# Head squares summed from a rounded and a low part, two places later in the projection

## The chip, the cores and the metric

One Trainium2 chip, one core of it. The metric is device time in microseconds (us) of that core from launch to end, the median of the runs shown. TensorE does matrix products into PSUM, VectorE and ScalarE do element-wise work, GpSimd does some more of it in SBUF alone, SyncE issues the DMAs. Each engine takes its instructions in the order in which they were written; semaphores order them against each other.

## The reference, cut to what matters

A trunk layer: a normalised and modulated input is projected to 20 tiles of 128 features. Four heads run a gated linear attention forward and backward, beside a short convolution and a pooling. The sum of both directions, `o` (128 features for each of 1024 tokens and each head), is normalised over its own 128 features and gated. Then come the output projection and a large MLP.

```
def gla_out(o, r, norm_w):
    o = o * lax.rsqrt(jnp.mean(o * o, axis=-1, keepdims=True) + EPS) * norm_w.astype(jnp.float32)
    bsz, h, n, dv = o.shape
    o = o.transpose(0, 2, 1, 3).reshape(bsz, n, h * dv)
    return (o * jax.nn.silu(r.astype(jnp.float32))).astype(r.dtype)
```

The change is in how the mean of `o * o` is made.

## The kernel before

Features lie on the partitions, tokens along the free dimension. All large products are made of rounded operands: `a_hi` and `w_hi` are copies rounded to the format F32R, `a_lo` and `w_lo` are what the rounding left, and a product is `w_hi*a_hi + w_hi*a_lo + w_lo*a_hi`. ScalarE makes `w_hi` for the next weight tile (L1540), VectorE makes `w_lo` (L2149).

The projection runs over the tiles of `PROJ` (L957), one tile of 128 features after the other, each over 8 contraction blocks. A block is six matmuls of 128x512: three products for each half of the tokens. The results alternate between the two halves of the PSUM tensor `main`. Into this stream a table, `PLAN`, puts the small work: `put(tile, slot, job)` runs a job behind contraction block `slot` of tile `tile`. I number these places as 8 x tile + slot. Every engine walks through the same table and issues its own part of each job, so one table sets the order of TensorE, ScalarE and VectorE. Three rules matter here. At the start of its tile ScalarE rounds the next weights, ahead of the tile's jobs; at slot 3 VectorE makes their low part, ahead of the slot's jobs; and behind the last job of a tile each engine works on what the tile itself made (for a gate tile `R` on ScalarE: L1708, L1709, L1710; for `CC` L1700; on VectorE for `CH` L2318 to L2323).

The jobs, with their lines:
- `A`, head and half: scores. TensorE L1127 into `sm`; VectorE masks them (L2212) and adds both directions to `a_sum` (L2218).
- `O`: outputs of a head and a half. TensorE L1149 and L1154 into `ob`. ScalarE squares `ob` once both halves are there (L1629), into `sqo`.
- `ns`, head and half: the sum of squares over the 128 features, spread over all partitions, as one FP32 product of 128x128 ones with 512 tokens of `sqo` (TensorE L1161, into `sm`). ScalarE makes the inverse root as exponential of a logarithm (L1488 reads `sm` and frees it, L1494). VectorE multiplies the outputs by it, once for both halves (L2224).
- `u`: state updates (TensorE L1109; ScalarE copies them out of `sm`, L1611, L1613). `ch`: VectorE's chain over the forward states (L2203). GpSimd runs the backward chain (L828, L831), outside the table. `mx`: ScalarE scales the states (L1620) that `O` reads.
- `pl`: the pooling's small product (TensorE L1168; ScalarE L1640). Its input `ypool` is finished by GpSimd (L853, L854).
- `rl`, `rg`: the gate. VectorE L2333, ScalarE's sigmoid L1714, then VectorE L2339 and L2341.

The tensor `sm` has two banks, used in turn by all these jobs in the order of the table; a job may write a bank only after the job two before it has been read (`begin_small`). The outputs of a head also wait for the multiplication of the head before (`y_normed`).

Head `h` has its outputs at `OUT_AT[h]` = 80, 96, 113, 124 and two places later. GpSimd's input for the pooling product of places 86 and 87 is made in tile 10, which is that of head 0's outputs.

Of the kernel before, what the change touches and what calls it, by code (L numbers as in the profile page):

```python
# [21 lines left out]
P = 128  # L22
# [109 lines left out]
for _h in range(HEADS):  # L132
    put_all(CHAIN_AT[_h], 2, ("ch", _h, 0), ("ch", _h, 1), ("ch", _h, 2))
    put_all(MIX_AT[_h], 1, ("mx", _h, 0), ("mx", _h, 1))
    for _d in range(2):
        put_all(HEAD_AT[_h], 2, ("A", _h, 0, _d), ("A", _h, 1, _d))
    put_all(OUT_AT[_h], 2, ("O", _h, 0), ("O", _h, 1))
    put_all(OUT_AT[_h] + 4, 1, ("ns", _h, 0), ("ns", _h, 1))
    _r = PROJ.index(f"R{_h}") + 1
    put(_r, 3, "rl", _h)  # L140
    put(_r, 5, "rg", _h)
    if _h >= 2:
        for _n in range(2):
            put_all(UPD_AT[_h], 2, ("u", _h, _n), ("u", _h, 2 + _n))
# [57 lines left out]
def hybrid_trunk(nc, wstream, wg_in, wm1, wm2, xt, ct, small_in, gw_in, out):  # L202
    ctx = ExitStack()
    with ctx:
        cursor = [(nc.sbuf_base + 63) // 64 * 64]

        def at(name, shape, dt, offset):
            return nc.alloc_sbuf_tensor_at(name, shape, dt, offset=offset)
# [94 lines left out]
        macc = at("macc", [P, N], F32, ZF + 5 * KIB)  # L303
        scaled_state = at("scaled_state", [P, DV], F32, ZF + 9 * KIB + 256)
        mbuf_late = at("mbuf_late", [P, 4, N], F32, ZD)
# [6 lines left out]
        sqo = at("sqo", [P, N], F32, ZF + 10 * KIB)  # L312
        rso = at("rso", [P, N], F32, ZF + 14 * KIB)

        early_hi = at("early_hi", [P, 2, N], F32R, ZA)
# [107 lines left out]
        o_done = sem("o_done")  # L423
        sqo_made = sem("sqo_made")
        rso_made = sem("rso_made")
        y_normed = sem("y_normed")
# [517 lines left out]
        def _(pe):  # L944
# [213 lines left out]
            def head_sums(h, i):  # L1158
                b = begin_small(("ns", h, i))
                pe.wait_ge(sqo_made, h + 1)  # L1160
                pe.matmul(sm[:, b, :], ones, sqo[:, i * HALF:(i + 1) * HALF], start=True, stop=True).then_inc(small_done, 1)  # L1161

# [319 lines left out]
        def _(act):  # L1482
# [140 lines left out]
            def outputs(h, i):  # L1623
                if i == 1:
                    act.wait_ge(o_done, 2 * (h + 1))
                    act.wait_ge(summed, 2)
                    if h >= 1:
                        act.wait_ge(y_normed, h)
                    act.activation(sqo[:, :], ob[:, :], ACT.Square).then_inc(sqo_made, 1)  # L1629

            def head_sums(h, i):
# [447 lines left out]
        def _(dve):  # L2079
# [141 lines left out]
            def head_sums(h, i):  # L2221
                if i == 1:
# [3 lines left out]
                    dve.wait_ge(y_normed, h + 1)  # L2226

            def mod_product(g):
                s = S_OF[("md", g)]
# [6 lines left out]

            jobs = {"ch": chain_states, "A": scores, "ns": head_sums, "md": mod_product}

# [603 lines left out]
```

## Time and profile before

| | us |
|---|---|
| median of 3 runs | 1082.21 |
| lowest and highest | 1081.92, 1082.45 |
| span of the profiled execution | 1081.0 |
| TensorE matmuls in flight | 1056.2 (98%) |
| VectorE busy | 824.0 (76%) |
| ScalarE busy | 510.8 (47%) |
| GpSimd busy | 307.5 (28%) |

The span is from the first to the last instruction of one execution; the time of a run also has what lies around it. A matmul's duration in the trace includes its way through the array, so neighbours overlap: what one costs is read from the distance of starts. A row of the timeline merges neighbours of one kind; in brackets stands the idle time ahead of it and who ended it.

### The profile page before, as it was taken

Reading aid. Unit: us, or ns where it says so; the run is one execution under the profiler, and the core shown is the slowest. Engines: PE = TensorE matmul, PEld = TensorE weight load, DVE = VectorE, ACT = ScalarE, POOL = GpSimd, SP = SyncE. Lnnn points to the kernel's source line nnn. Section 1 sums busy time; section 2 is a strip of 40 time slices with the busy share of each in tenths; the row PEclk is TensorE's granted clock in tenths of the full one; section 3 lists DMA queues with packets and bytes.
Section 4 is the critical chain, followed back from the end, with each engine's and each line's share of the span. In section 5 each row is a group of like instructions: output and inputs, shape, how many; then the busy total and the mean of one; then the engine's idle time right before and its main releaser. Section 6 shows DMA issues by size and latency. Waiting matters only on the chain.

```text
span 1081.0 us, 16409 instructions
## 1 busy us (share of the span) xinstructions
PE 1056.2 (98%) x5566; PEld 850.7 (79%) x5566; DVE 824.0 (76%) x1062; ACT 510.8 (47%) x827; POOL 307.5 (28%) x280
## 2 busy tenths in 40 slices
PE   8999999999999999999999999999999999999995
PEld 4688888777778888887888888888788888888883
DVE  5878868646445986899787787878987777787776
ACT  6665443356525123576766666666422222222234
POOL 1000006487101452012332423233322231222222
PEclk9999999999999999999999999999999999999998
DMA  9733331101013664226766565768745854774604
GB/s 338 260 111 104 117 117 40 40 21 40 21 59 116 263 233 146 78 98 251 308 247 260 224 269 229 269 236 312 291 170 221 349 205 181 314 278 184 237 1 156
DMA packets 66646, 199.82 MB, mean 185 GB/s; under 512 B 5664, under 2 KB 15136, under 8 KB 66592
## 3 DMA queue, kind: packets, MB, share of 16 engines
q1 hardware_dynamic: 66592, 199.11, 49.7%
q8 instruction: 33, 0.54, 0.2%
q14 instruction: 21, 0.17, 0.0%
HBM read 139.32 MB, written 59.77 MB: 184 GB/s over the span
## 4 chain that ended last, share of the span: by engine, by line
PE 49%; DVE 4%; issue 1%; POOL 0%; DVEq 0%; ACT 0%; ACTq 0%; POOLq 0%
PE ob L1410 13%; PE main L1452 13%; PE sm L1410 10%; PE sm L1452 8%; PE ob L1452 6%; DVE XR L2680 1%; DVE XR L2747 1%; DVE stage L2561 1%; DVE slot L2511 1%; DVE slot L2506 0%; DVE stage_last L2561 0%; DVE t_tmp L2554 0%; DVE hid L2568 0%; DVE t_tmp L2545 0%; POOL raw L918 0%
## 5 line engine op out<-in xcount | busy, mean ns | idle before, releaser
L957 PE MATMUL main<-a_hi,w_hi 128*128 128x512 f32 x376 | 125.8, 416 | 0.0
L1410 PE MATMUL ob<-h_sum,slot 128*128 128x512 f32 x504 | 122.5, 392 | 2.3 <-DVE hid L2568 2.1
L1881 ACT ACTIVATE slot<-raw 128x512 fp32r<-128x512 f32 x80 | 50.2, 631 | 153.1 <-PE main L1452 58.4
L957 PE MATMUL main<-a_lo,w_hi 128*128 128x512 f32 x376 | 116.5, 391 | 0.0
L957 PE MATMUL main<-a_hi,w_lo 128*128 128x512 f32 x376 | 116.2, 390 | 0.0
L1410 PEld LDWEIGHTS ob<-h_sum,slot 128*128 128x128 f32 x504 | 95.2, 189 | 22.9 <-issue 2.5
L2680 DVE SCALAR_TENSOR_TENSOR XR<-main,mods,XR 128x512 f32<-128x512 f32 x112 | 83.3, 748 | 28.8 <-PE main L1452 27.7
L957 PEld LDWEIGHTS main<-a_lo,w_hi 128*128 128x128 f32 x376 | 70.6, 188 | 15.5
L957 PEld LDWEIGHTS main<-a_hi,w_lo 128*128 128x128 f32 x376 | 70.6, 188 | 15.5
L957 PEld LDWEIGHTS main<-a_hi,w_hi 128*128 128x128 f32 x376 | 66.7, 188 | 17.9 <-issue 5.8
L1452 PE MATMUL main<-t_even,slot 128*128 128x512 f32 x336 | 78.1, 389 | 0.0
L2506 DVE TENSOR_TENSOR slot<-raw,slot 128x512 fp32r<-128x512 f32 x70 | 62.5, 894 | 18.5 <-ACT slot L1869 18.5
L1410 PE MATMUL sm<-h_hi,slot 128*128 128x512 f32 x224 | 73.5, 389 | 0.0
L1452 PEld LDWEIGHTS main<-t_even,slot 128*128 128x128 f32 x336 | 63.1, 188 | 13.1
L828 POOL TENSOR_TENSOR scaled_state<-tst,decay 64x128 f32<-64x128 f32 x60 | 29.0, 483 | 146.2 <-ACT tst L1613 141.7
L2511 DVE TENSOR_TENSOR slot<-raw,slot 128x512 fp32r<-128x512 f32 x80 | 61.3, 781 | 0.2 <-ACT slot L1881 0.2
L2680 DVE SCALAR_TENSOR_TENSOR XR<-sm,mods,XR 128x512 f32<-128x512 f32 x64 | 47.7, 748 | 13.3 <-PE sm L1452 12.4
L918 POOL TENSOR_TENSOR raw<-part_sum,raw 128x512 f32<-128x512 f32 x16 | 21.0, 1312 | 122.3 <-DVE slot L2511 122.3
L889 POOL TENSOR_TENSOR held<-raw 128x512 f32<-128x512 f32 x14 | 23.3, 1663 | 108.4 <-DMA raw<-wstream 60.3
L897 POOL TENSOR_TENSOR held<-raw 128x512 f32<-128x512 f32 x14 | 24.6, 1756 | 90.9 <-DVE slot L2506 90.9
L2680 DVE SCALAR_TENSOR_TENSOR XR<-ob,mods,XR 128x512 f32<-128x512 f32 x48 | 35.8, 749 | 18.4 <-PE ob L1452 18.3
L1410 PEld LDWEIGHTS sm<-h_hi,slot 128*128 128x128 f32 x224 | 42.1, 188 | 8.7
(338 smaller groups left out, 2442.1 us busy)
## 6 DMA issues: line engine op xcount, KB each, us to landing
hidden_kept<-stage SPq DMA_DIRECT2D x98, 512.0 KB, 4.3
raw<-wstream SPq DMA_DIRECT2D x60, 512.0 KB, 4.2
t_even<-hidden_kept SPq DMA_DIRECT2D x56, 512.0 KB, 5.7
raw<-wstream SPq DMA_DIRECT2D x16, 1024.0 KB, 5.4
stage<-hidden_kept SPq DMA_DIRECT2D x21, 512.0 KB, 5.5
stage_last<-hidden_kept SPq DMA_DIRECT2D x21, 512.0 KB, 6.4
wmod<-wm SPq DMA_DIRECT2D x8, 1024.0 KB, 12.8
mbuf<-wm SPq DMA_DIRECT2D x16, 512.0 KB, 4.0
```

The lines of the kernel that those rows point to most:

```text
L828: pool.tensor_tensor(scaled_state[DK:P, :], tst[DK:P, h % 2, c, :], decay[DK:P, h, c:c + 1].broadcast_to([DK, DV]), ALU.mult).then_inc(sta ...
L889: pool.tensor_tensor(sums, a21, a22, ALU.add).then_inc(w1_sum, 1)
L897: pool.tensor_tensor(sums, a12, a11, ALU.subtract).then_inc(w1_sum, 1)
L918: pool.tensor_tensor(a11, sums, a11, ALU.subtract).then_inc(w2_sum, 1)
L957: ins = pe.matmul(main[:, bank, half * HALF:(half + 1) * HALF], w[:, slot, k, :], x[:, half * HALF:(half + 1) * HALF], start=begin, stop=end)
L1410: ins = pe.matmul(hid_bank(acc, odd), slots1[j][:, w, kp, :], parts[x][:, kp, :], start=PARTS[j][3] and kp == 0 and m == 0, stop=kp == KP ...
L1452: ins = pe.matmul(product_bank(s, acc, q), slots2[j][:, w, q, kp, :], tset[odd][j][kp][:, x, :], start=begins and kp == 0 and n == 0, stop ...
L1881: act.activation(slots2[j][:, 0, :, :, :], operand(s, j), ACT.Copy).then_inc(w2_hi, 1)
L2506: tt(slots1[j][:, 1, :, :], operand1(b, j), slots1[j][:, 0, :, :].bitcast(F32), ALU.subtract).then_inc(w1_lo, 1)
L2511: tt(slots2[j][:, 1, :, :, :], operand(s, j), slots2[j][:, 0, :, :, :].bitcast(F32), ALU.subtract).then_inc(w2_lo, 1)
L2561: tt(y[:, 1, :], sources(odd)[j], y[:, 0, :].bitcast(F32), ALU.subtract).then_inc(t_lo, 1)
L2680: stt(out=XR[m][:, cols], in0=product_bank(s, acc, q), scalar=mods[:, 3, m:m + 1], in1=XR[m][:, cols], op0=ALU.mult, op1=ALU.add).then_inc ...
```

## The change

Per head, three things change.

1. The squares are split as the other operands are. ScalarE rounds `sqo` to `sqo_hi`, right behind the squares. VectorE makes `sqo_lo = sqo - sqo_hi` in a new job, `sl`, at the place where the first sum used to be. In head 0 ScalarE also rounds the ones once (`ones_r`).
2. A sum is two products of `ones_r`, with `sqo_hi` and with `sqo_lo`, in place of one FP32 product.
3. The two sums of a head move two places later: from 84, 85 / 100, 101 / 117, 118 / 128, 129 to 86, 87 / 102, 103 / 119, 120 / 130, 131. ScalarE's and VectorE's parts of `ns` move with them.

`sqo_lo` lies where `sqo` lies and `sqo_hi` where the inverse root is written later; the ones take a place beside GpSimd's `scaled_state`, which moves by 256 bytes. No DMA is added or moved.

```diff
-    put_all(OUT_AT[_h] + 4, 1, ("ns", _h, 0), ("ns", _h, 1))
+    put_all(OUT_AT[_h] + 4, 1, ("sl", _h))
+    put_all(OUT_AT[_h] + 6, 1, ("ns", _h, 0), ("ns", _h, 1))
...
-                pe.wait_ge(sqo_made, h + 1)
-                pe.matmul(sm[:, b, :], ones, sqo[:, i * HALF:(i + 1) * HALF], start=True, stop=True).then_inc(small_done, 1)
+                pe.wait_ge(sqo_split, h + 1)
+                cols = slice(i * HALF, (i + 1) * HALF)
+                pe.matmul(sm[:, b, :], ones_r[:, :], sqo_hi[:, cols], start=True, stop=False)
+                pe.matmul(sm[:, b, :], ones_r[:, :], sqo_lo[:, cols], start=False, stop=True).then_inc(small_done, 1)
...
                     act.activation(sqo[:, :], ob[:, :], ACT.Square).then_inc(sqo_made, 1)
+                    act.wait_ge(sqo_made, h + 1)
+                    if h == 0:
+                        act.activation(ones_r[:, :], ones, ACT.Copy)
+                    act.activation(sqo_hi[:, :], sqo[:, :], ACT.Copy).then_inc(sqo_rounded, 1)
...
+            def square_low(h):
+                dve.wait_ge(sqo_rounded, h + 1)
+                tt(sqo_lo[:, :], sqo[:, :], sqo_hi[:, :].bitcast(F32), ALU.subtract).then_inc(sqo_split, 1)
```

TensorE in head 0, from the second of its output products on, before. A row `L957` with `x2` is a third of a contraction block; numbers in names are those of the allocation.

```order
L1161 MATMUL sm<-sqo_114,small_65 128x512 [waits sqo_made,small_free0]
L957 MATMUL main<-a_hi_52,w_hi_50 128x512 x2
L957 MATMUL main<-a_lo_53,w_hi_50 128x512 x2
L957 MATMUL main<-a_hi_52,w_lo_51 128x512 x2
L1161 MATMUL sm<-sqo_114,small_65 128x512 [waits sqo_made,small_free1]
...
L1168 MATMUL sm<-ypool_99,small_65 128x512 [waits masks_loaded,pooled,small_free0]
...
L1168 MATMUL sm<-ypool_99,small_65 128x512 [waits masks_loaded,pooled,small_free1]
```

And after, the same stretch:

```order
L1168 MATMUL sm<-sqo_hi_118,ones_r_107 128x512 [waits sqo_split,small_free0]
L1169 MATMUL sm<-sqo_lo_117,ones_r_107 128x512
L1176 MATMUL sm<-ypool_99,small_65 128x512 [waits masks_loaded,pooled,small_free1]
...
L1168 MATMUL sm<-sqo_hi_118,ones_r_107 128x512 [waits sqo_split,small_free0]
L1169 MATMUL sm<-sqo_lo_117,ones_r_107 128x512
L1176 MATMUL sm<-ypool_99,small_65 128x512 [waits masks_loaded,pooled,small_free1]
```

The sums used to stand one and two blocks ahead of the pooling products; now a sum stands directly in front of each.

ScalarE in head 2, from its squares on, before:

```order
L1629 ACTIVATE sqo_114<-ob 128x1024 [waits y_normed,summed,o_done]
L1714 ACTIVATE rsig_113<-rsig_113 128x1024 [waits r_min]
L1488 ACTIVATE rso_115<-sm,small_65 128x512 [waits small_done]
L1494 ACTIVATE rso_115<-rso_115 128x512 [waits small_free0]
L1488 ACTIVATE rso_115<-sm,small_65 128x512 [waits small_done]
L1494 ACTIVATE rso_115<-rso_115 128x512 [waits small_free1]
L1708 ACTIVATE rsig_113<-main 128x1024 [waits y_gated,pads_made,tile_done]
L1709 ACTIVATE rsig_113<-rsig_113 128x1024 [waits act_chain]
L1710 ACTIVATE rsig_113<-rsig_113,small_65 128x1024 [waits act_chain]
L1540 ACTIVATE w_hi_50<-raw_49 128x1024 [waits split_done,tile_done,raw_loaded0]
```

And after:

```order
L1637 ACTIVATE sqo_115<-ob 128x1024 [waits y_normed,summed,o_done]
L1641 ACTIVATE sqo_hi_118<-sqo_115 128x1024 [waits sqo_made]
L1726 ACTIVATE rsig_114<-rsig_114 128x1024 [waits r_min]
L1496 ACTIVATE rso_116<-sm,small_65 128x512 [waits small_done]
L1502 ACTIVATE rso_116<-rso_116 128x512 [waits small_free0]
L1720 ACTIVATE rsig_114<-main 128x1024 [waits y_gated,pads_made,tile_done]
L1721 ACTIVATE rsig_114<-rsig_114 128x1024 [waits act_chain]
L1722 ACTIVATE rsig_114<-rsig_114,small_65 128x1024 [waits act_chain]
L1548 ACTIVATE w_hi_50<-raw_49 128x1024 [waits split_done,tile_done,raw_loaded0]
L1496 ACTIVATE rso_116<-sm,small_65 128x512 [waits small_done]
L1502 ACTIVATE rso_116<-rso_116 128x512 [waits small_free1]
```

The second logarithm stands behind the gate's three operations and the rounding of the next weights; the new rounding stands in front of the sigmoid.

VectorE in head 1, from the last piece of its forward chain on, before:

```order
L2203 SCALAR_TENSOR_TENSOR tst_101<-tst_101,decay_69 64x128 [waits states_forward] x4
L2149 TENSOR_TENSOR w_lo_51<-raw_49,w_hi_50 128x1024 [waits hi_made]
L2224 TENSOR_TENSOR vtok_92<-ob,rso_115 128x8x128 [waits rso_made]
L2327 TENSOR_TENSOR yconv_100<-main,yconv_100 128x1024 [waits tile_done,y_normed]
```

And after:

```order
L2215 SCALAR_TENSOR_TENSOR tst_101<-tst_101,decay_69 64x128 [waits states_forward] x4
L2161 TENSOR_TENSOR w_lo_51<-raw_49,w_hi_50 128x1024 [waits hi_made]
L2242 TENSOR_TENSOR sqo_lo_117<-sqo_115,sqo_hi_118 128x1024 [waits sqo_rounded]
L2236 TENSOR_TENSOR vtok_92<-ob,rso_116 128x8x128 [waits rso_made]
L2343 TENSOR_TENSOR yconv_100<-main,yconv_100 128x1024 [waits tile_done,y_normed]
```

The low part of the squares stands behind the low part of the weights. In head 2 it stands behind the gate (L2355, L2357 after, L2339 and L2341 before).

## Rows read from the trace of the kernel before

**Rows 1.** The page: span, and TensorE's busy time.
```profile
span 1081.0 us, 16409 instructions
PE 1056.2 (98%) x5566; PEld 850.7 (79%) x5566; DVE 824.0 (76%) x1062; ACT 510.8 (47%) x827; POOL 307.5 (28%) x280
```

**Rows 2.** Timeline of TensorE, head 0: start, duration, line, operands, count, idle before.
```profile
208.85 0.62 PE L957 MATMUL main<-a_hi,w_hi 128*128 128x512 f32 x2
...
210.23 1.04 PE L1161 MATMUL sm<-sqo,small 128*128 128x512 f32 x2
...
214.74 1.02 PE L1168 MATMUL sm<-ypool,small 128*128 128x512 f32 x2
```

**Rows 3.** Timeline of ScalarE, head 0 and the state copies behind it.
```profile
209.00 1.03 ACT L1629 ACTIVATE sqo<-ob 128x1024 f32<-128x1024 f32 x1 [7.29 <-DVE ypool L2311]
...
218.04 0.69 ACT L1640 ACTIVATE ypool<-sm,small 128x512 f32<-128x512 f32 x1 [1.56 <-PE sm L1168]
...
222.83 0.59 ACT L1613 ACTIVATE tst<-sm 64x512 f32<-64x512 f32 x1
```

**Rows 4.** Timeline of GpSimd: the pooling's last operation, two of the chain.
```profile
212.50 2.02 POOL L854 TENSOR_TENSOR ypool<-ypool,upad 128x1024 f32<-128x1024 f32 x1
...
247.11 1.47 POOL L828 TENSOR_TENSOR scaled_state<-tst,decay 64x128 f32<-64x128 f32 x1
...
249.19 0.40 POOL L828 TENSOR_TENSOR scaled_state<-tst,decay 64x128 f32<-64x128 f32 x1
```

**Rows 5.** Timeline of TensorE, head 1: outputs, first sum, state products.
```profile
234.95 0.69 PE L1149 MATMUL ob<-a_sum,vtok 64*64 64x64 f32 x32 [0.18 <-ACT tst L1620]
...
244.19 1.02 PE L1161 MATMUL sm<-sqo,small 128*128 128x512 f32 x2
...
248.79 1.16 PE L1109 MATMUL sm<-vtok,ktok 64*128 64x128 f32 x16
...
252.82 1.16 PE L1109 MATMUL sm<-vtok,ktok 64*128 64x128 f32 x16
```

**Rows 6.** Timeline of VectorE, head 1.
```profile
236.84 0.69 DVE L2218 TENSOR_TENSOR a_sum<-a_f,a_b 128x512 f32<-128x512 f32 x1 [2.43 <-PE ob L1154]
...
247.10 1.21 DVE L2149 TENSOR_TENSOR w_lo<-raw,w_hi 128x1024 fp32r<-128x1024 f32 x1
```

**Rows 7.** Timeline of TensorE, heads 2 and 3: first sums, scores between.
```profile
280.28 1.10 PE L1161 MATMUL sm<-sqo,small 128*128 128x512 f32 x2 [0.97 <-ACT sqo L1629]
...
286.31 0.69 PE L1127 MATMUL sm<-qe,ku 64*64 64x64 f32 x32
...
302.71 1.02 PE L1161 MATMUL sm<-sqo,small 128*128 128x512 f32 x2
```

**Rows 8.** Timeline of ScalarE, head 2.
```profile
279.13 1.00 ACT L1629 ACTIVATE sqo<-ob 128x1024 f32<-128x1024 f32 x1
280.04 1.04 ACT L1714 ACTIVATE rsig<-rsig 128x1024 f32<-128x1024 f32 x1
281.41 0.69 ACT L1488 ACTIVATE rso<-sm,small 128x512 f32<-128x512 f32 x1 [0.33 <-PE sm L1161]
...
285.05 1.03 ACT L1708 ACTIVATE rsig<-main 128x1024 f32<-128x1024 f32 x1
...
288.26 1.04 ACT L1540 ACTIVATE w_hi<-raw 128x1024 fp32r<-128x1024 f32 x1
```

**Rows 9.** Timeline of VectorE, the gates behind heads 2 and 3.
```profile
282.37 1.28 DVE L2341 SCALAR_TENSOR_TENSOR vtok<-vtok,small,rsig 128x1024 f32<-128x1024 f32 x1
...
300.81 1.29 DVE L2341 SCALAR_TENSOR_TENSOR vtok<-vtok,small,rsig 128x1024 f32<-128x1024 f32 x1
```

**Rows 10.** Stretches: busy time by engine (count), then TensorE's granted clock, DMA.
```profile
1070.00:1072.00 2.00, 0.00 (x0) 0.00 (x0) 2.00 (x5) 1.12 (x2) 0.80 (x1) 1.00 1.03 382
1072.00:1075.00 3.00, 0.00 (x0) 0.00 (x0) 2.66 (x5) 1.44 (x2) 1.70 (x2) 0.56 1.01 382
```

More of the change, by code:

```diff
@@ L303, in hybrid_trunk @@
         macc = at("macc", [P, N], F32, ZF + 5 * KIB)
-        scaled_state = at("scaled_state", [P, DV], F32, ZF + 9 * KIB + 256)
+        scaled_state = at("scaled_state", [P, DV], F32, ZF + 9 * KIB)
+        ones_r = at("ones_r", [P, P], F32R, ZF + 9 * KIB + 512)
         mbuf_late = at("mbuf_late", [P, 4, N], F32, ZD)
@@ L313, in hybrid_trunk @@
         rso = at("rso", [P, N], F32, ZF + 14 * KIB)
+        sqo_lo = at("sqo_lo", [P, N], F32R, ZF + 10 * KIB)
+        sqo_hi = at("sqo_hi", [P, N], F32R, ZF + 14 * KIB)
         early_hi = at("early_hi", [P, 2, N], F32R, ZA)
@@ L424, in hybrid_trunk @@
         sqo_made = sem("sqo_made")
+        sqo_rounded = sem("sqo_rounded")
+        sqo_split = sem("sqo_split")
         rso_made = sem("rso_made")
@@ L2235, in mod_product @@
                     link(stt(out=gain2[:, :], in0=mods[:, 2, :], scalar=1.0, in1=col("n2"), op0=ALU.add, op1=ALU.mult))
-            jobs = {"ch": chain_states, "A": scores, "ns": head_sums, "md": mod_product}
+            jobs = {"ch": chain_states, "A": scores, "sl": square_low, "ns": head_sums, "md": mod_product}
             def gates(j):
```

## The prediction

> **What bounds the kernel now.** I read the head of the page first: the span is 1081.0 us and TensorE has matmuls in flight for 98% of it [rows 1]. So matmul time is time, and every wait put in front of TensorE is time too, unless a wait behind it shrinks. Everything the change touches lies between 205 and 310 us, so I then read TensorE's timeline there. A contraction block of the projection (six rounded matmuls) takes 210.23 - 208.85 = 1.38 us, thus a pair of rounded 128x512 matmuls 1.38 / 3 = 0.46. From 210.23 to 214.74 stand two blocks and two FP32 sums, so an FP32 128x512 matmul costs (4.51 - 2 x 1.38) / 2 = 0.87 [rows 2]. Last I read ScalarE, VectorE and GpSimd in the same stretch [rows 3, 4, 6, 8, 9], because the new operands of the sums come from two of them, through queues that run in order. All times below are on the trace's axis; a "shift" is how much later TensorE is than before.
>
> **What it removes.** Eight FP32 sums, 8 x 0.87 = 7.0 us on TensorE's path. It adds eight pairs of rounded ones, 8 x 0.46 = 3.7. Alone that is 8 x 0.41 = 3.3 us faster. The one wait for the squares that the trace has, 0.97 us in head 2 [rows 7], could go as well.
>
> **What it adds.** Per head: a ScalarE copy that rounds the squares, 1.04 us (the copy of a weight tile has the same shape [rows 8]), in head 0 also the rounding of the 128x128 ones (no such row: above 0, below the 0.69 of a 128x512 operation [rows 8]; I take 0.3, and it decides nothing below); then a VectorE subtraction, 1.22 us by the low part of the weights, same shape and types [rows 6]. The last is queued at the first of the four places, the sums two places later, so TensorE gives the chain 2 x 1.38 us more. The question is per head whether both queues are free by then.
>
> **Head 0 (places 84 to 87).** The squares run from 209.00 to 210.03 [rows 3], the ones to about 210.35, the rounded squares to 211.35, the low part to 212.6. TensorE without the sums comes to place 86 at 210.23 + 2 x 1.38 = 213.0: no wait for the sum. But at the same place the pooling product follows, and TensorE now asks for it at 213.5 instead of 214.74. Its input comes from GpSimd, whose last operation on it runs from 212.50 for 2.02 us, to 214.52 [rows 4]: a wait of 1.1 us that the two FP32 sums had covered. And VectorE's subtraction reads two SBUF tensors while GpSimd works. Such a subtraction (247.10, 1.21 us [rows 6]) stretched the GpSimd operation beside it from 0.40 to 1.47 us [rows 4], so I take 1.1 us more: input ready at 215.6, product at 215.7, shift +1.0. With one sum (0.46) now between the two pooling products the second stands at 215.7 + 0.87 + 1.38 + 0.46 = 218.4. ScalarE copies it out behind its own logarithm and exponential of the sum: sum done 218.57, then 0.69 + 0.66, so the copy starts at 219.9 instead of 218.04 [rows 3]. From there ScalarE has no gap to 222.83 + 0.59 = 223.42, where TensorE's state product waits for its banks, so that product shifts by +1.85. The output product of head 1 had a wait of 0.2 us of its own (234.95 [rows 5]), whose releaser, GpSimd's chain, moves by only 1.1: the wait vanishes. Shift there: +1.6.
>
> The Trainium skill, GPSIMD Engine Reference, section 8 (Key points), says that GpSimd shares its SBUF interfaces with VectorE and that VectorE instructions with two SBUF inputs contend. The rows of 247.10 agree; by this rule the shift at the pooling product is +1.0, and without it -0.1, which makes the whole sum about 1.1 us smaller.
>
> **Head 1 (places 100 to 103).** VectorE's queue is what is late. From 236.84, when the first output product frees it, it works without a gap to the low part of the weights at 247.10 [rows 6], and the new subtraction stands behind that one: 248.24 to 249.46. TensorE comes to place 102 at 244.19 + 2.76 = 246.95 [rows 5], so it waits 2.5 us, to 249.5. Behind the sum at this place are the state products, for which ScalarE must first have read the sum's bank: 249.5 + 0.62 + 0.03 + 0.69 (logarithm [rows 8]) = 250.85, where TensorE is free at 250.06: 0.8 us more. They start at 250.9; the next ones follow after 252.82 - 248.79 = 4.03 us [rows 5] plus the second sum, 0.46: 255.4 instead of 252.82, +2.6. Shift: +4.2. GpSimd's chain for head 2's outputs starts on those products, so it moves along.
>
> **Head 2 (places 117 to 120).** On the axis of before: squares at 279.13 to 280.13 (ScalarE is late from the scaled states, whose chain moves along), rounded squares to 281.2, then the sigmoid of the first gate, which was at 280.04 [rows 8], from 281.1 to 282.15. VectorE gates head 0 behind that (its first operation lies between 281.08 and 282.37, its second ends at 283.65 [rows 9]), now +1.07: 284.7. Only then comes the subtraction, to 285.9. TensorE, at place 117 at 280.28 - 0.97 = 279.31, comes to 119 at 282.1: a wait of 3.8 us. Worse is the split over two tiles: the sum of place 119 is the last job of its tile, that of place 120 the first of the next. ScalarE's order has the three gate operations and the rounding of the next weights between their logarithms (shown word for word in the section on the change). They took from 285.05 to 289.30 [rows 8]. Now: first sum at 285.9, logarithm and exponential to 287.9, the block of 4.25 us to 292.0, second logarithm to 292.65. TensorE issued the second sum at 287.7, and directly behind it stands the score product of head 3, which needs that bank: from 288.3 it waits 4.4 us, to 292.7 instead of 286.31 [rows 7]. Shift: +6.4.
>
> **Head 3 (places 128 to 131).** Squares at about 299.9, rounded by 302.1; VectorE's gate ends at 302.10 [rows 9], low part by 303.3. TensorE comes to place 130 at 302.71 + 2.76 = 305.5 [rows 7]: no wait, and 2 x 0.41 = 0.8 us are gained.
>
> **Sum.** 1.6 + 2.6 + 6.4 - 0.8 = +9.8 us. After that TensorE is the bound again, and what is later on it is later at the end. Against the profiled execution's own span: 1081.0 + 9.8 = 1090.8. The median of the runs shown, 1082.21, lies 1.2 above that span; so **1092.0 us**, +0.9%.
>
> **Rivals.**
> *All of it stays covered* (faster). The low part would have to be written before TensorE reaches the sum in every head, and the second logarithm before the score product. Then -3.3, with head 2's wait gone -4.3: 1078 to 1079. For it: the lead of two places, 2.76 us, is longer than either new operation, and heads 0 and 3 keep it. Against it: the queues above. It decides at 246.95 in head 1 (VectorE is busy to 248.3) and at 282.1 in head 2. 4%.
> *GpSimd is not held up by the new subtraction.* Head 0 then costs 0.5 instead of 1.6: 1090.9. 15%.
> *Only one of head 2's waits counts*: if the second logarithm finds ScalarE free, 4.4 us fall away: 1087.6. The order speaks against it. 7%.
> *The clock falls.* The end of the trace has TensorE idle: the granted clock is still 1.00 (2.4 GHz) in the two us from 1070, 0.56 on average in the three from 1072, with no matmul in either [rows 10]. Head 2's two waits, 3.8 and 4.4 us, are the first such gaps between matmuls in this kernel. A fall in the first costs nothing, since the 2.3 us of work up to the second would be hidden by it at 1.2 GHz too; one in the second costs 1.38 us for each contraction block run at half clock. How many those are no row shows; one to four give 1.4 to 5.5, I take 2: 1094. 29%. The Trainium skill, TensorE: Matmul & The Clock Gate, section Why this matters for your kernels, says that idle gaps between bursts of matmuls bring the half clock back. No row inside the kernel tests it. By that rule this rival's 1094 would be the forecast, by the trace's middle 1092.
>
> **Numbers.** The forecast of 1092.0 has 45%, as GpSimd held, both of head 2's waits, no fall. The range must hold the GpSimd and the clock cases and a size of ScalarE's block that is off by a microsecond: 1088.5 to 1095.5; it leaves out the covered case, the one-wait case and the top of the clock case. A difference of 0.2% (2.2 us) is about what a measurement of this kernel can tell from none. Slower 0.93, within 0.02, faster 0.05.
>
> **What would show it.** In the profile after: rounded sums at 0.46 us a pair; a TensorE wait of 1 to 2.5 us on GpSimd's pooling in head 0; one of about 2.5 on VectorE's low part and one of 0.8 on a logarithm in head 1; 3.8 and 4.4 in head 2, the second released by ScalarE's logarithm; none in head 3. TensorE's matmul time should be 3.3 us less and its idle time some 13 us more. I am wrong if VectorE reaches the low part of head 1 before 247 us, if ScalarE makes the second logarithm of head 2 before the gate block, or if the wait for the banks was already there in another form.

## The result and the profile after

The changed kernel takes **1098.01 us** (median of 4 runs, 1096.19 to 1098.84), beside 1082.18 (1081.92 to 1082.45) for the kernel before in the same comparison: a ratio of 1.0143, 95% interval 1.0132 to 1.0155. That is 15.8 us slower, where +9.8 was forecast: the sign was right, the size lies outside the range. The profiled execution is the one of 1096.19; its span is 1094.4, 13.4 longer than that of before.

The page of the changed kernel: the span, busy time by engine, and the granted clock of TensorE in 40 slices.

```profile
span 1094.4 us, 16417 instructions
...
PE 1059.1 (97%) x5566; PEld 854.7 (78%) x5566; DVE 830.2 (76%) x1066; ACT 514.4 (47%) x832; POOL 309.5 (28%) x280
...
PEclk9999999999799999999999999999999999999998
```

The forecast was 3.3 us less matmul time than in [rows 1]. There are 2.9 more, and one slice (the eleventh, 274 to 301 us) has a clock of 0.7. TensorE's idle time, span less busy, went from 24.8 to 35.3. So two things are to be found: which waits came, and where the clock went.

The waits of the changed kernel between 130 and 340 us: who waited for whom, the sum, how often, the longest.

```profile
DVE rsig L2355 <- ACT rsig L1726: 8.2, 2, 7.1
...
PE sm L1168 <- DVE sqo_lo L2242: 7.1, 3, 4.0
...
PE sm L1133 <- issue: 2.8, 1, 2.8
...
PE sm L1115 <- issue: 1.3, 2, 0.8
```

TensorE waits three times for the low part of the squares. "issue" says that the profile shows no releaser; the order tells it (a bank that ScalarE has to read first). The wait of VectorE's gate in it, 7.1 us at the longest, comes back below. Now the same places as in [rows 2, 5, 7]: TensorE's timeline after, heads 0 to 3 (start, duration, line, operands, count, idle before).

```profile
213.32 0.47 PE L1168 MATMUL sm<-sqo_hi,ones_r 128*128 128x512 f32 x1 [0.56 <-DVE sqo_lo L2242]
213.62 0.39 PE L1169 MATMUL sm<-sqo_lo,ones_r 128*128 128x512 f32 x1
213.86 1.02 PE L1176 MATMUL sm<-ypool,small 128*128 128x512 f32 x2
...
235.23 0.69 PE L1155 MATMUL ob<-a_sum,vtok 64*64 64x64 f32 x32 [0.47 <-ACT tst L1628]
...
249.88 0.47 PE L1168 MATMUL sm<-sqo_hi,ones_r 128*128 128x512 f32 x1 [2.52 <-DVE sqo_lo L2242]
...
251.40 1.23 PE L1115 MATMUL sm<-vtok,ktok 64*128 64x128 f32 x16 [0.82 <-issue]
...
290.69 0.77 PE L1168 MATMUL sm<-sqo_hi,ones_r 128*128 128x512 f32 x1 [4.00 <-DVE sqo_lo L2242]
...
298.06 1.13 PE L1133 MATMUL sm<-qe,ku 64*64 64x64 f32 x32 [2.77 <-issue]
...
319.68 0.39 PE L1168 MATMUL sm<-sqo_hi,ones_r 128*128 128x512 f32 x1
319.90 0.39 PE L1169 MATMUL sm<-sqo_lo,ones_r 128*128 128x512 f32 x1
```

The difference of starts to [rows 5, 7] is the shift: the first output product of head 1 is 0.28 late, the scores of head 3 are 11.75 late (298.06 against 286.31). In head 3 the two rounded products of a sum start 0.22 apart and nothing waits. Who holds the low part in heads 1 and 2 stands in VectorE's timeline after.

```profile
247.39 1.21 DVE L2161 TENSOR_TENSOR w_lo<-raw,w_hi 128x1024 fp32r<-128x1024 f32 x1
248.52 1.21 DVE L2242 TENSOR_TENSOR sqo_lo<-sqo,sqo_hi 128x1024 fp32r<-128x1024 f32 x1
...
286.86 1.22 DVE L2355 TENSOR_TENSOR rsig<-main,rsig 128x1024 f32<-128x1024 f32 x1 [7.05 <-ACT rsig L1726]
288.12 1.28 DVE L2357 SCALAR_TENSOR_TENSOR vtok<-vtok,small,rsig 128x1024 f32<-128x1024 f32 x1
289.33 1.22 DVE L2242 TENSOR_TENSOR sqo_lo<-sqo,sqo_hi 128x1024 fp32r<-128x1024 f32 x1
```

In head 1 it stands behind the low part of the weights, in head 2 behind the gate. VectorE had stood still 7.05 us for ScalarE's sigmoid, so it was not busy there, only queued in the wrong order. And who holds the scores of head 3: ScalarE's timeline after, between the two logarithms of head 2.

```profile
291.92 0.69 ACT L1496 ACTIVATE rso<-sm,small 128x512 f32<-128x512 f32 x1 [5.09 <-PE sm L1169]
...
293.17 1.00 ACT L1720 ACTIVATE rsig<-main 128x1024 f32<-128x1024 f32 x1
...
296.35 1.04 ACT L1548 ACTIVATE w_hi<-raw 128x1024 fp32r<-128x1024 f32 x1
297.30 0.67 ACT L1496 ACTIVATE rso<-sm,small 128x512 f32<-128x512 f32 x1
```

The second logarithm ends at 297.97, and the scores start at 298.06. Last the clock: stretches of the changed kernel, with busy time of TensorE, its weight loads, VectorE, ScalarE and GpSimd, then the granted clock (1.00 is 2.4 GHz, 0.50 is 1.2) and DMA.

```profile
253.00:255.00 2.00, 2.00 (x6) 1.52 (x6) 0.00 (x0) 1.86 (x4) 0.00 (x0) 0.50 0.00 0
...
256.00:260.00 4.00, 4.00 (x29) 3.12 (x28) 2.39 (x2) 3.57 (x6) 0.00 (x0) 1.00 0.00 0
286.00:290.00 4.00, 0.69 (x4) 0.22 (x2) 3.10 (x3) 0.83 (x1) 0.00 (x0) 0.99 0.00 0
290.00:300.00 10.00, 6.54 (x44) 4.89 (x45) 1.85 (x3) 6.58 (x8) 0.00 (x0) 0.50 0.00 0
300.00:303.00 3.00, 3.00 (x8) 2.32 (x8) 2.08 (x3) 0.00 (x0) 0.00 (x0) 0.50 0.00 0
...
304.00:310.00 6.00, 6.00 (x112) 4.81 (x112) 1.89 (x3) 0.00 (x0) 0.00 (x0) 1.00 0.01 3
```

It fell twice. Behind head 1's gaps (2.52, then 0.82) it was at half for some three microseconds, when TensorE was at work again: the contraction block at 252.56 took 2.73 us instead of 1.38. In head 2 it fell at the end of the first gap and stayed at half through the second one and some five microseconds beyond the start of the scores (298.06; 0.50 to 303). The forecast had named such a fall as a rival, in head 2 only, at 2 us.

A span also holds what differs ahead of the change. The last wait of TensorE that no kernel here alters (0.80 us, for the masks) ends at 196.04 in the kernel before and at 195.69 in the changed one, and between 195.65 and 196.86 in those below. So I also give, for each kernel, how much later than before TensorE comes to the first matmul of the MLP (439.88 us in the kernel before), counted from the end of that wait: its lateness, 13.7 us in the changed kernel. It comes from one execution, as a span does, but it leaves out what differs ahead of the change and in the MLP.

### The profile page after: what moved, and what is told of

Read it like the earlier page. It is cut to its first block, busy times and chain, and to the rows that moved or that the text cites. A ratio compares the mean times of both kernels' runs of the same rounds, so it can differ in the third digit from the quotient of the medians.

```text
span 1094.4 us, 16417 instructions
## 1 busy us (share of the span) xinstructions
PE 1059.1 (97%) x5566; PEld 854.7 (78%) x5566; DVE 830.2 (76%) x1066; ACT 514.4 (47%) x832; POOL 309.5 (28%) x280
## 4 chain that ended last, share of the span: by engine, by line
PE 48%; DVE 4%; issue 1%; POOL 0%; DVEq 0%; ACT 0%; ACTq 0%; POOLq 0%
PE ob L1418 13%; PE main L1460 12%; PE sm L1418 10%; PE sm L1460 8%; PE ob L1460 5%; DVE XR L2696 1%; DVE XR L2763 1%; DVE stage L2577 1%; DVE slot L2527 1%; DVE slot L2522 0%; DVE stage_last L2577 0%; DVE t_tmp L2570 0%; DVE hid L2584 0%; DVE t_tmp L2561 0%; DVE t_tmp L2556 0%
## 5 line engine op out<-in xcount | busy, mean ns | idle before, releaser
L963 PEld LDWEIGHTS main<-a_lo,w_hi 128*128 128x128 f32 x376 | 71.7, 191 | 15.8
L818 POOL TENSOR_TENSOR w_hi<-raw,small 128x1024 fp32r<-128x1024 f32 x7 | 18.6, 2651 | 112.0 <-PE main L963 112.0
```

The costliest lines, as they stand in the source:

```text
L818: pool.tensor_tensor(w_hi[:, b, :, :], raw[:, b, :, :], ones.unsqueeze(1).broadcast_to([P, KT, P]), ALU.mult).then_inc(linked, 1)
L963: ins = pe.matmul(main[:, bank, half * HALF:(half + 1) * HALF], w[:, slot, k, :], x[:, half * HALF:(half + 1) * HALF], start=begin, stop=end)
```

## The experiments

The theory, **A**: the waits are those of the prediction (VectorE's order in heads 1 and 2, and ScalarE's between the two logarithms of head 2), and what is missing to 1098 is the price of the clock. The rival, **B**: the waits are longer in themselves, or work behind them is slower for another reason than the clock. The changed kernel and the ten of the experiments, each with the ratio to the kernel before as run beside it on the same chip. Span and lateness are those of the one profiled execution:

| kernel | what it is | median us (range, runs) | ratio (95%) | span | lateness |
|---|---|---|---|---|---|
| after | the change | 1098.01 (1096.19-1098.84, 4) | 1.0143 (1.0132-1.0155) | 1094.4 | 13.7 |
| e1_filled | spare matmuls in three waits | 1091.48 (1090.64-1091.94, 4) | 1.0074 (1.0057-1.0091) | 1090.2 | 9.0 |
| e8_fill_head2 | the same in head 2 alone | 1094.80 (1091.64-1095.26, 4) | 1.0107 (1.0089-1.0124) | 1092.6 | 10.6 |
| e2_move_only | places moved, no split | 1086.85 (1086.29-1088.34, 5) | 1.0034 (1.0019-1.0048) | 1086.5 | 6.2 |
| e3_split_only | split, places not moved | 1099.92 (1099.30-1101.21, 4) | 1.0157 (1.0139-1.0174) | 1097.9 | 17.5 |
| e5_head2_together | both sums of head 2 in one tile | 1090.93 (1088.01-1091.77, 4) | 1.0070 (1.0053-1.0087) | 1089.9 | 9.0 |
| e9_head1_only | low part of head 1 earlier | 1091.58 (1090.20-1092.76, 4) | 1.0084 (1.0066-1.0102) | 1089.3 | 8.5 |
| e10_head2_low_first | low part of head 2 ahead of the gate | 1091.82 (1090.83-1094.23, 4) | 1.0082 (1.0065-1.0099) | 1092.4 | 11.7 |
| e6_head1_low_early | both of these | 1087.97 (1087.85-1088.48, 4) | 1.0051 (1.0036-1.0066) | 1086.7 | 5.2 |
| e4_replaced | all places chosen by the queues | 1081.88 (1080.10-1083.91, 10) | 0.9993 (0.9983-1.0003) | 1078.7 | -0.8 |
| e7_mixed | as e4, head 0 in FP32 as before | 1080.95 (1079.67-1082.06, 11) | 0.9986 (0.9977-0.9995) | 1079.1 | -1.4 |

**Filling the waits.** The same dependences, but TensorE works in the long waits on products that nobody reads (into the bank that the next sum overwrites). Ten in head 1, 16 in head 2's first wait, 18 ahead of the scores of head 3.

```diff
-                banks = [begin_small(("A", h, i, e)) for e in range(2)]
+                banks = [begin_small(("A", h, i, 0))]
+                if h == 3 and i == 0:
+                    for _ in range(18):
+                        pe.matmul(sm[:, banks[0], :], a_hi[:, 0, 0:P], a_hi[:, 0, 0:HALF], start=True, stop=True)
+                banks.append(begin_small(("A", h, i, 1)))
...
+                if i == 0:
+                    for _ in range({1: 10, 2: 16}.get(h, 0)):
+                        pe.matmul(sm[:, b, :], a_hi[:, 0, 0:P], a_hi[:, 0, 0:HALF], start=True, stop=True)
```

> The changed kernel, with spare matmuls (rounded, 128x512, 0.23 us each, into a bank that is overwritten afterwards) where TensorE only waits: 10 ahead of head 1's first sum, 16 ahead of head 2's, 18 between head 2's second sum and head 3's scores. They add no work to the path if the waits are as long as in the profile after (2.5 and 4.0 us, and 4.4 by the prediction's sum at full clock). Theory A (waits plus a fallen clock): the granted clock stays 1.00 through 245 to 310 us and the time falls by what the half clock cost, 4.6 us of the profiled execution's 13.4 and up to 7 of the median's 15.8: about 1091. Rival B (waits alone, and they are longer than I summed them): the time stays at 1096 to 1098.

Measured: 1091.48, with a ratio of 1.0074 against 1.0143. The first sums of heads 1 and 2 and the scores of head 3 in its TensorE timeline:

```profile
250.25 0.50 PE L1175 MATMUL sm<-sqo_hi,ones_r 128*128 128x512 f32 x1 [0.16 <-DVE sqo_lo L2249]
...
289.45 0.50 PE L1175 MATMUL sm<-sqo_hi,ones_r 128*128 128x512 f32 x1 [0.30 <-DVE sqo_lo L2249]
...
296.34 0.69 PE L1137 MATMUL sm<-qe,ku 64*64 64x64 f32 x32 [0.25 <-ACT rso L1503]
```

And the stretch with head 2 of the same kernel (columns as above):

```profile
280.00:300.00 20.00, 19.45 (x116) 15.20 (x119) 6.56 (x7) 12.24 (x21) 0.00 (x0) 1.00 0.01 4
```

The sums still come when the low part is there (250.25 beside 249.88), so no dependence was shortened; all that changed is that TensorE did not stand still. The clock stays at 1.00, and 4.7 us of lateness (4.2 of span) and 6.5 of the median are gone (7.5 by the ratios). B is out for that part: more useless work made the kernel faster. The price of the clock is 4.7 us between the two profiled executions. The 6.5 to 7.5 over the runs are more than these two gaps are shown to cost: three of the four executions of the filled kernel have a mean granted clock of 0.997, its profiled one 0.994, which fits a fall in the MLP that comes and goes (see the part on the forecast). What is left, 8.0 us by the ratio, 8.8 by the medians of that comparison and 9.0 of lateness, is the price of the waits themselves. The Trainium skill, TensorE: Matmul & The Clock Gate, section Why this matters for your kernels, says that idle stretches between bursts of matmuls bring half the clock back; this pair of kernels agrees.

**Filling head 2 alone** tells what head 1's fall costs (the difference to the filled kernel).

```diff
-                    for _ in range({1: 10, 2: 16}.get(h, 0)):
+                    for _ in range({2: 16}.get(h, 0)):
```

> The changed kernel with spare matmuls in head 2's two waits only (16 and 18), none in head 1's. Theory A (each fall of the clock has its own price): head 1's fall stays, 0.50 from about 252.3 to 255.6 us, and costs 1.7; head 2's goes. 1091.5 + 1.7 = 1093.2. Rival B (only head 2's fall matters): 1091.5.

Measured: 1094.80. Its waits are 2.50, 0.82, 0.30 and 0.25. The stretches with head 1 and with all that follows:

```profile
250.00:262.00 12.00, 10.16 (x58) 7.99 (x59) 3.32 (x3) 8.51 (x15) 3.29 (x6) 0.86 0.13 45
280.00:345.00 65.00, 64.45 (x507) 52.15 (x506) 27.53 (x26) 28.27 (x42) 0.13 (x1) 1.00 0.13 44
```

Against the fully filled kernel head 1's fall costs 1.6 us of lateness, where 1.7 was expected, and head 2's then 3.1. (The spans say 2.4 and 1.8, but at 196 us already this kernel was 0.7 later than the filled one and 1.2 later than the changed one.) The medians say 3.3 and 3.2 (3.6 by the ratios for each). Both falls count. That the medians are above the traces is not explained: the four executions of this kernel lie between 1091.64 (clock 0.997) and 1095.26 (0.991), so a difference of two such medians is rough.

**The move alone**: FP32 sums as before, two places later (the difference to the kernel before).

```diff
-    put_all(OUT_AT[_h] + 4, 1, ("ns", _h, 0), ("ns", _h, 1))
+    put_all(OUT_AT[_h] + 6, 1, ("ns", _h, 0), ("ns", _h, 1))
```

> The kernel before with FP32 sums as they were, but two places later; no split. Theory A (the place in the two queues costs, not the split's work): head 1's state products wait 0.8 us for the logarithm; in head 2 the second logarithm stands behind the gate block, TensorE waits about 4 us in front of head 3's scores, minus the 0.97 that goes; +3.8 us, and 1.7 to 2.5 more if the clock falls in that gap: 1086 to 1088.5. Rival B (only the split costs, moving is harmless): 1081 to 1082.

Measured: 1086.85, as expected. Its one large wait:

```profile
289.72 1.13 PE L1127 MATMUL sm<-qe,ku 64*64 64x64 f32 x32 [3.94 <-issue]
```

And the stretch behind it:

```profile
290.00:295.00 5.00, 5.00 (x42) 4.01 (x38) 3.39 (x4) 0.28 (x1) 0.00 (x0) 0.50 0.00 0
```

So the places 119 and 120, one tile apart, make a wait of 3.94 us without any split, and the clock falls behind it. In head 1 only the wait of 0.82 for the sum's bank is left, and the clock stays at 1.00 there.

**The split alone**, the sums at their old places (the difference to the changed kernel, as in the following ones unless said).

```diff
-    put_all(OUT_AT[_h] + 6, 1, ("ns", _h, 0), ("ns", _h, 1))
+    put_all(OUT_AT[_h] + 4, 1, ("ns", _h, 0), ("ns", _h, 1))
```

> The changed kernel with the sums at their old places, the low part at the first of them. Theory A (the low part is ready when the queues allow it, whatever the place of the sum): TensorE waits 2.9, 5.3 and 6.6 us in heads 0, 1 and 2 and 0.6 in head 3 and has no wait for the second logarithm; with 3.3 of work and 0.97 of wait gone +11 us, plus 2 to 5 for falls of the clock: 1095 to 1098. Rival B (the lead of two places is what hurts, by the banks and the logarithms): 1080 to 1084.

Measured: 1099.92, two above the upper end. The waits for the low part in its TensorE timeline:

```profile
213.24 0.47 PE L1168 MATMUL sm<-sqo_hi,ones_r 128*128 128x512 f32 x1 [3.25 <-DVE sqo_lo L2242]
...
253.00 0.77 PE L1168 MATMUL sm<-sqo_hi,ones_r 128*128 128x512 f32 x1 [5.03 <-DVE sqo_lo L2242]
...
296.83 0.77 PE L1168 MATMUL sm<-sqo_hi,ones_r 128*128 128x512 f32 x1 [6.72 <-DVE sqo_lo L2242]
```

The one in head 3 is 0.61. By the ratios the split costs 17.0 us where it stood, the move 3.7 without it, and both together 15.5. The two places that the chain was given are worth 5.2 us to it (17.0 + 3.7 - 15.5), and the move takes 3.7 of these back. The waits are as expected: 15.6 in sum, less 3.3 of work and 0.97 of wait, is 11.3 beside the 11 of the expectation. The lateness is 17.5, so some 6 are left for the clock (an estimate), above the 2 to 5 that were allowed. It fell behind the 3.25 in head 0 as well (0.93 on average from 205 to 230, where the changed kernel has 1.00). No run isolates that fall.

**Head 2's sums in one tile** removes the split over two tiles.

```diff
+LOW_PLACE = (84, 100, 117, 128)
+SUM_PLACE = ((86, 87), (102, 103), (119, 119), (130, 131))
...
-    put_all(OUT_AT[_h] + 4, 1, ("sl", _h))
-    put_all(OUT_AT[_h] + 6, 1, ("ns", _h, 0), ("ns", _h, 1))
+    put_all(LOW_PLACE[_h], 1, ("sl", _h))
+    for _i in range(2):
+        put_all(SUM_PLACE[_h][_i], 1, ("ns", _h, _i))
```

> The changed kernel, but head 2's two sums both at place 119, the last of their tile; nothing else moves. Theory A (ScalarE's order): the second logarithm now stands ahead of the gate block, the wait in front of head 3's scores shrinks from 4.4 us (by the sum at full clock) to about 0.4, the wait of 4.0 for the low part stays. Waits and work 4 to 4.5 us less, and the stretch of half clock behind the first gap is no longer prolonged: 1090 to 1092. Rival B (the gap in front of the scores has another cause, the masks or the outputs): 1096 to 1098.

Measured: 1090.93. The wait of 4.05 for the low part stays, the one ahead of the scores is gone, and 7.9 us with it (by the ratios; 4.7 of lateness). That is more than the wait of 2.77: the work between the two waits was hidden by ScalarE's block and is no longer, but the half-clock stretch is shorter too (0.66 from 290 to 300, 1.00 from there). The second sum itself moves one block ahead too, but it was not what the scores waited for: in the changed kernel it ends as their wait of 2.77 begins. Its logarithm now stands ahead of the gate block. This settles who released them.

**Head 1's low part earlier**, at place 97, ahead of a piece of VectorE's chain. I first ran it with a sort rule that puts every low part first in its place. This moved head 2's ahead of the gate as well, which I had not seen: the kernel holds two edits, not one.

Against the experiment before:

```diff
-LOW_PLACE = (84, 100, 117, 128)
+LOW_PLACE = (84, 97, 117, 128)
...
-    _jobs.sort(key=lambda job: (job[0] != "O"))
+    _jobs.sort(key=lambda job: (job[0] not in ("O", "sl")))
```

(The sums are at their places of the changed kernel.)

> The changed kernel, but head 1's low part at place 97, ahead of VectorE's last piece of the forward chain; the sums stay at 102 and 103. Theory A (VectorE's queue): the wait of 2.5 us goes, the 0.8 for the logarithm stays, the clock no longer falls behind it (1.7 us less): 1093 to 1094, TensorE's granted clock 1.00 from 240 to 280 us. Rival B (a gap of 0.8 is enough for the clock, or the low part is late for ScalarE's sake): 1095 or more.

Measured: 1087.97, a miss by five or more. The two edits were then taken apart, with these sort rules:

```diff
+    _jobs.sort(key=lambda job: (job[0] != "O" and job != ("sl", 1)))
```

> The changed kernel with one thing moved: head 1's low part at place 97, ahead of VectorE's last piece of the forward chain. (The earlier experiment of that aim also put head 2's low part ahead of the gate at place 117, by its rule for the order within a place.) Theory A (each head's wait has its own cause in VectorE's queue): head 1's wait of 2.5 us and the fall of the clock behind it (1.7) go, head 2's wait of 4.0 stays: 1098.0 - 4.2 = 1093.8. Rival B (the earlier experiment's 10 us came from head 1 alone): 1088.

```diff
+    _jobs.sort(key=lambda job: (job[0] != "O" and job != ("sl", 2)))
```

> The changed kernel with one thing moved: at place 117 head 2's low part stands ahead of the gate on VectorE. Theory A: the wait for it shrinks from 4.0 to 0.65 us, 0.4 more waits for the gate's bank, the gap in front of the scores stays (4.1 us, ScalarE's gate block), with one fall of the clock behind it instead of the long one of 13 us: 5.8 us less, 1092.2; head 1's wait of 2.5 and its fall stay. Rival B (the gap in front of the scores takes over what is gained): 1096 or more.

(In the first of the two the low part of head 1 is at 97, in the second at 100 as in the change.) Measured: 1091.58 and 1091.82. Head 2 in the TensorE timeline of e10:

```profile
288.73 0.47 PE L1168 MATMUL sm<-sqo_hi,ones_r 128*128 128x512 f32 x1 [0.61 <-DVE sqo_lo L2242]
289.86 0.70 PE L963 MATMUL main<-a_hi,w_hi 128*128 128x512 f32 x2 [0.43 <-DVE rsig L2355]
...
296.06 1.13 PE L1133 MATMUL sm<-qe,ku 64*64 64x64 f32 x32 [4.12 <-issue]
```

Taking the low part out from behind the gate shortens the first wait from 4.00 to 0.61. Yet the first sum starts only 2.0 earlier than in the changed kernel (288.73 against 290.69), because TensorE came to it 1.4 later, mostly by head 1, where the clock stood low for six microseconds and not for three (shown in the last section). ScalarE's block starts with that sum, so the scores come 2.0 earlier as well, and the wait in front of them grows from 2.77 to 4.12. Of the expected 5.8 this execution shows 2.0. That the median met the expectation is luck as far as the trace goes: the other three executions are 1.8 to 3.4 shorter. Their mean granted clocks order them, 1090.83 at 0.994, 1091.21 at 0.992, 1092.42 at 0.990, and the profiled 1094.23 at 0.988.

In e9 the wait of 2.5 is gone, the waits of head 2 are the old ones (4.01 and 2.77), and yet it came 2.2 below the expectation. The clock in its head 2:

```profile
285.00:290.00 5.00, 3.45 (x8) 2.81 (x9) 1.40 (x2) 2.19 (x3) 0.00 (x0) 0.50 0.00 0
...
292.00:294.00 2.00, 0.08 (x5) 0.11 (x8) 0.00 (x0) 1.97 (x4) 0.00 (x0) 1.00 0.00 0
...
295.00:298.00 3.00, 3.00 (x9) 2.32 (x8) 2.90 (x4) 0.00 (x0) 0.00 (x0) 0.50 0.00 0
```

Here it came back within the second gap and fell again for some three microseconds, where in the changed kernel it was down without a break. The same two gaps had another price: from head 2's outputs to head 3's TensorE falls back by 8.7 us here and by 9.6 in the changed kernel. The expectation had taken head 2's price from the changed kernel's profile; that step does not hold. Nor does the rival that head 1 alone gave the 10 us. By the medians the two edits give 6.4 and 6.2 alone and 10.0 together (by lateness 5.2, 2.0 and 8.5), so they do not simply add up, in either measure.

**All places by the queues.** The low part goes where VectorE is free (84, 97, 116, 128), both sums of head 1 to 101 and both of head 2 to 119, and a low part goes first in its place (the rule of e6). The two tables against the changed kernel:

```diff
+LOW_PLACE = (84, 97, 116, 128)
+SUM_PLACE = ((86, 87), (101, 101), (119, 119), (130, 131))
```

> The changed kernel with other places: the low part of head 1 at 97, ahead of VectorE's last piece of the forward chain, that of head 2 at 116, ahead of the gate; both sums of head 1 at 101, ahead of the state products, both of head 2 at 119, so that both logarithms stand ahead of the gate block. Theory A (queues): waits of 0.6 and 0.35 in head 1, 0.35 and 0.4 in head 2, head 0 as after (+0.6), 3.3 of work and 0.97 of wait gone, clock never below 1.00: about 1081. Rival B (the split is dear wherever it stands, by VectorE's and ScalarE's work): 1088 or more.

Measured: 1081.88 (ratio 0.9993). Six waits of 0.25 to 0.66 are left (2.99 in sum), and the clock is at 1.00 in this stretch. TensorE comes to the MLP 0.8 us early, and the median shows 0.8. The span is 2.3 shorter, but 0.3 of that was there at 196 us and 1.1 comes in the MLP, where this execution lacks a fall of the clock that the profiled one of before has. Three of the six waits are head 0's, so in the last kernel head 0 was left as it was. Against this kernel, with head 0 left out of ScalarE's and VectorE's new parts too:

```diff
+SUM_PLACE = ((84, 85), (101, 101), (119, 119), (130, 131))
...
+                if h == 0:
+                    pe.wait_ge(sqo_made, 1)
+                    pe.matmul(sm[:, b, :], ones, sqo[:, cols], start=True, stop=True).then_inc(small_done, 1)
+                    return
```

> The places of the experiment before that put the low parts early and the sums of heads 1 and 2 together, but head 0 as in the kernel before: one FP32 product, at 84 and 85, no split. Theory A (in head 0 the VectorE subtraction and GpSimd's pooling hold each other up, 0.6 us more than the 0.8 that the rounded sums save there): about 0.6 us below that experiment, span about 1078.1, time about 1081, 0.1% faster than before. Rival B (head 0 is neutral): the same as that experiment, or 0.8 above it, if head 0's saving is real and its waits are absorbed.

Measured: 1080.95, ratio 0.9986 (0.9977 to 0.9995), the fastest of all, 1.4 us below the kernel before and little more than can be told from no change. It comes to the MLP 1.4 early, 0.65 ahead of e4, as theory A has it for head 0. The spans of the two (1079.1 and 1078.7) say the opposite only because this execution is 1.1 later at 196 us already, and the ratios overlap. Its whole stretch from 195 to 345:

```profile
195.00:345.00 150.00, 147.47 (x1317) 115.46 (x1316) 83.29 (x97) 75.28 (x126) 63.55 (x97) 1.00 0.15 54
```

## Why the forecast had the sign and not the size

**What it removes** (-3.3): right. In head 3, where nothing waits, the rounded products start 0.22 to 0.23 apart, and TensorE's shift falls from 14.25 to 13.35, by 0.9 where 0.8 was forecast.

**Head 0** (+1.6): wrong, it is +0.6 (0.28 on the axis, where the squares had started 0.35 earlier than in [rows 3]). The step that failed is "its input comes from GpSimd, whose last operation on it runs from 212.50". That operation works for the second group of pooling. GpSimd in the changed kernel:

```profile
196.52 2.36 POOL L860 TENSOR_TENSOR ypool<-ypool,upad 128x1024 f32<-128x1024 f32 x1
...
212.17 2.88 POOL L860 TENSOR_TENSOR ypool<-ypool,upad 128x1024 f32<-128x1024 f32 x1
```

The product at 213.86 started while the second of these ran (to 215.05); its input was there since 198.88. The kernel says so too: a pooling product waits for `pooled` to reach `i + 1`, and at places 86 and 87 `i` is 0, the first group. (In GpSimd's own order that group belongs to tile 10, as the section on the kernel before has it; in time it was done before head 0's first outputs.) I had taken the nearest operation by time and name. [rows 2] could not have told, since the product before started at 214.74, behind both. The hold-up itself was right (2.88 against 2.02 in [rows 4]), nobody waited for it. What came in its place were 0.56 for the low part, 0.48 at the state products and 0.47 at head 1's outputs.

**Head 1** (+2.6; waits 2.5 and 0.8): the waits are 2.52 and 0.82. The fall of the clock behind them was not in the step: 1.35 us in one block of this execution, 1.6 in all by e8.

**Head 2** (waits 3.8 and 4.4): 4.00 and 2.77. The second is shorter because TensorE did the work between the two at half clock and came later; it did not end earlier, as the forecast says of its clock rival. On the axis the scores start at 298.06, where the forecast's steps give 286.31 + 6.4 + 4.2 = 296.9. ScalarE's queue was read right, operation for operation.

**Head 3** (no wait, -0.8): right, and the last difference of 13.4 is there by the end.

**The clock** is the step that failed: the forecast's sum put it at nothing, and filling the waits gave 4.7 us back. The rival had the mechanism, but "I take 2" was too small, "head 2's two waits are the first such gaps" left out head 1's, "A fall in the first costs nothing" is not so (0.7 up to the scores), and at 29% it was not in the forecast. In the profiled execution: 9.8 forecast, +0.45 to head 2 (head 0 gives 1.0 back and the execution is 0.35 ahead from the start, head 1's fall takes more), +0.7 up to the scores (the sum and its logarithm start later at half clock), +2.5 behind them (the shift grows from 11.75 to 14.25 until the next output product), which makes 13.4. At full clock the steps are right in their sum: 9.8 less head 0's 1.0 is 8.8, and the filled kernel has 9.0 of lateness, +8.8 by the medians and 8.0 by its ratio. That one of these is equal to a tenth is luck.

"No row inside the kernel tests it" was wrong as well. Its rows stop at 310 us and go on at 1070. In between the trace of before has a gap and a fall of the clock behind it:

```profile
504.30 4.20 PE L1410 MATMUL ob<-h_sum,slot 128*128 128x512 f32 x12 [2.07 <-DVE hid L2568]
...
505.80:509.10 3.30, 3.30 (x9) 2.59 (x8) 3.27 (x5) 3.27 (x7) 0.71 (x1) 0.50 0.57 210
```

So a gap of 2.07 us had brought half clock in the kernel before, and head 1's forecast wait of 2.5 was longer. But the fall is not certain. The changed kernel and the ten of the experiments have this gap too (2.06 to 2.11 us, in e5 and e8 2.97). Three of them have no fall behind it, e4, e7 and e5:

```profile
514.32 2.98 PE L1421 MATMUL ob<-h_sum,slot 128*128 128x512 f32 x12 [2.97 <-DVE hid L2587]
...
514.40:530.00 15.60, 15.36 (x67) 12.40 (x68) 14.97 (x23) 12.33 (x23) 4.26 (x3) 1.00 0.90 327
```

The same twelve matmuls took 4.20 us with the fall and 2.98 without.

**What stays open.** The median is 1.8 above the profiled execution, which was the lowest of the four. In e10 the longer executions have the lower mean clock, and in the kernel before those at 0.996 and 0.997 have spans about 1 us shorter than those at 0.993 to 0.995 (medians among the 15 runs beside e5). That fits the fall at 504, there in some executions and not in others, but those runs have no profile. It does not carry over to the changed kernel: the profiled execution has 0.986 and the other three 0.986 and 0.987, so a longer time at half clock is not what their 1.8 us show. The cause of these is open. Nor do the runs tell why a stretch at half clock was 3 us long in one place and 13 in another, or why the same gap brings it in one execution and not in the next.

## To carry to other kernels

Where engines run their queues in order, an operation put between two engines costs what stands ahead of it in the queue, not its own 1.2 us; ask for each moved job what it now stands behind, and whether a pair that shares banks was cut apart by a block of other work. A wait of some microseconds put in front of a TensorE that was hardly idle has two prices, the wait and half the clock behind it, and the second was here larger than the saving sought. So place the new operation by the queues first (here 16 us lay between two placements of the same instructions), check what an operation waits for in the kernel before pricing a wait on it, and look for gaps and falls of the clock in the whole trace of before, not only where the change acts.

## What the runs showed of the hardware

**The clock after gaps.** Between 196 and 345 us it fell in or behind gaps of 2.5 + 0.8, of 3.25, 3.94, 4.0, 4.1 and 5.0 to 6.7; it did not where no wait was over 0.97 (head 2 of before, e4, e7, and head 1 of e2, e6 and e9). In the MLP (503 to 521 us) it fell behind a gap of 2.06 to 2.11 in eight profiles and of 2.97 in e8, and did not behind the same gaps in e4, e7 and e5 (2.08, 2.06 and 2.97; the rows of e5 are in the part on the clock). In head 1 of the changed kernel it fell some 2.5 us after TensorE had resumed (249.88; 0.68 on average from 252 to 253, 0.50 behind that), and the stretch at half was between 3 us (head 1 of the changed kernel) and 13 (head 2), for gaps that differ much less. Head 1 of e10 had the same waits (2.49 and 0.82) and was down for six:

```profile
251.00:257.00 6.00, 5.18 (x24) 4.29 (x24) 0.00 (x0) 4.08 (x8) 1.61 (x4) 0.50 0.09 38
```

**VectorE and GpSimd hold each other up, both ways.** In head 0 the subtraction beside GpSimd's pooling took 2.17 us instead of 1.22, and the pooling operation 2.88 instead of 2.02. In head 1 only GpSimd paid: an operation of 0.40 us was held over both subtractions, to 2.60 (1.47 over one, [rows 4]), and these took 1.21 each. VectorE's timeline of the changed kernel, head 0:

```profile
211.00 2.17 DVE L2242 TENSOR_TENSOR sqo_lo<-sqo,sqo_hi 128x1024 fp32r<-128x1024 f32 x1 [1.19 <-ACT sqo_hi L1641]
```

And GpSimd's, in head 1:

```profile
247.39 2.60 POOL L834 TENSOR_TENSOR scaled_state<-tst,decay 64x128 f32<-64x128 f32 x1
```

The prediction had only GpSimd's side of it. The Trainium skill, GPSIMD Engine Reference, section 8 (Key points), tells of contention with VectorE instructions that have two SBUF inputs; the rows agree.
